# One wide matmul for both activation parts in the up projections, and a whole PSUM bank for each output chunk

## The reference

```python
# block 1: D_FF = 8192
u = _rmsnorm(h, norm_mlp_g[layer])
a = jnp.einsum('bsd,df->bsf', u, w_up[layer])
a = jnp.square(jax.nn.relu(a))
h = h + jnp.einsum('bsf,fd->bsd', a, w_down[layer])

# block 2: D_FF_2 = 5504 = 43 * 128
u = jnp.einsum('btd,df->btf', h, w_up)
u_gate, u_val = jnp.split(u, 2, axis=-1)
g = lax.conv_general_dilated(u_gate.reshape(b, rows, cols, D_FF_2), conv_w[:, :, None, :], ...)  # 3x3 depthwise
g = g.reshape(b, t, D_FF_2) + conv_b
return jnp.einsum('btf,fd->btd', jax.nn.silu(g) * u_val, w_down)
```

## Time and profile before

| | |
|---|---|
| median of 3 runs | 2585.89 us (2580.50 to 2589.67) |
| the profiled execution: its own time | 2585.03 us |
| the profiled execution: span from first to last instruction | 2583.3 us |
| PE busy | 2503.9 us, 97% of the span |
| DVE busy | 1671.1 us, 65% |
| ACT busy | 1080.1 us, 42% |
| DMA | 532.2 MB, mean 206 GB/s |

### The profile page before, as it was taken

The page is one execution under the profiler, slowest core; times in us unless marked ns, Lnnn a source line. Parts: engine busy times, 40 slices in busy tenths (PEclk is TensorE's granted clock), DMA queues, the critical chain, the costliest instruction groups (busy, mean ns, idle before and its releaser), DMA issues.

```text
span 2583.3 us, 36773 instructions
## 1 busy us (share of the span) xinstructions
PE 2503.9 (97%) x14876; PEld 2198.4 (85%) x14876; DVE 1671.1 (65%) x2051; ACT 1080.1 (42%) x1318; POOL 0.2 (0%) x4
## 2 busy tenths in 40 slices
PE   8998999999999999999899999889899999999997
PEld 6886789899899899878678887678899889988996
DVE  5434587867877876654158745766677657775675
ACT  5434544343434344554154444334433434333333
POOL 0000000000000000000000000000000000000000
PEclk9999999999999999999999999989999999999999
DMA  7661567887887887556649866016466665666563
GB/s 281 193 194 49 195 236 265 286 275 275 285 279 269 285 279 258 166 170 191 225 160 354 316 194 208 1 58 189 122 184 181 186 203 182 181 184 188 182 181 127
DMA packets 133365, 532.20 MB, mean 206 GB/s; under 512 B 14944, under 2 KB 14944, under 8 KB 121840
## 3 DMA queue, kind: packets, MB, share of 16 engines
q1 hardware_dynamic: 133232, 530.31, 62.7%
HBM read 528.16 MB, written 2.10 MB: 205 GB/s over the span
## 4 chain that ended last, share of the span: by engine, by line
PE 92%; DVE 5%; ACT 1%; issue 1%; DMA 1%; ACTq 0%; SPq 0%; DVEq 0%
PE PSA L568 28%; PE PSA L570 28%; PE PSA L569 28%; PE PSA L693 1%; DVE cv L1486 1%; PE PSA L1016 1%; PE PSA L724 1%; PE PSA L736 1%; DVE XX L1779 1%; PE PSA L577 0%; PE PSA L1017 0%; PE PSA L904 0%; DVE wlo L1516 0%; PE PSA L871 0%; PE PSA L855 0%
## 5 line engine op out<-in xcount | busy, mean ns | idle before, releaser
L1516 DVE TENSOR_TENSOR wlo<-raw,whi 128x1024 fp32r<-128x1024 f32 x788 | 927.8, 1218 | 423.5 <-ACT whi L1096 420.5
L1096 ACT ACTIVATE whi<-raw 128x1024 fp32r<-128x1024 f32 x788 | 798.3, 1052 | 576.1 <-DMA raw<-in_w_down 212.3
L568 PE MATMUL PSA<-uhi,whi 128*128 128x256 f32 x2400 | 679.5, 283 | 1.0 <-DVE ulo L1629 1.0
L569 PE MATMUL PSA<-ulo,whi 128*128 128x256 f32 x2400 | 679.2, 283 | 0.0
L570 PE MATMUL PSA<-uhi,wlo 128*128 128x256 f32 x2400 | 679.2, 283 | 0.0
L568 PEld LDWEIGHTS PSA<-uhi,whi 128*128 128x128 f32 x2400 | 460.8, 192 | 1.4 <-DVE ulo L1629 1.2
L569 PEld LDWEIGHTS PSA<-ulo,whi 128*128 128x128 f32 x2400 | 460.8, 192 | 0.2
L570 PEld LDWEIGHTS PSA<-uhi,wlo 128*128 128x128 f32 x2400 | 460.7, 192 | 0.0
L568 PE MATMUL PSA<-whi,uhi 128*128 128x512 f32 x1088 | 429.2, 395 | 3.2 <-DVE zl L1879 2.2
L569 PE MATMUL PSA<-wlo,uhi 128*128 128x512 f32 x1088 | 427.0, 392 | 0.0
L570 PE MATMUL PSA<-whi,ulo 128*128 128x512 f32 x1088 | 426.8, 392 | 0.0
(11 more groups left out here) (275 smaller groups left out, 1531.0 us busy)
## 6 DMA issues: line engine op xcount, KB each, us to landing
raw<-in_w_up SPq DMA_DIRECT2D x300, 512.0 KB, 3.6
raw<-in_w_in SPq DMA_DIRECT2D x208, 512.0 KB, 3.9
raw<-in_w_down SPq DMA_DIRECT2D x192, 512.0 KB, 3.6
mod_slot<-in_w_mod_rows SPq DMA_DIRECT2D x78, 1024.0 KB, 6.2
raw<-in_w_out SPq DMA_DIRECT2D x64, 512.0 KB, 3.6
raw<-in_w_mod SPq DMA_DIRECT2D x36, 512.0 KB, 4.4
raw<-in_w_down2b SPq DMA_DIRECT2D x20, 512.0 KB, 3.9
h<-in_x SPq DMA_DIRECT2D x2, 1024.0 KB, 6.1
```

What stands on the lines that cost most here:

```text
L568: pe.matmul(dst, xh, wh, start=start, stop=False)
L569: pe.matmul(dst, xh, wl, start=False, stop=False)
L1096: AF(whi[:, n % SLOTS, 0:w], raw[:, n % SLOTS, 0:w], ACT.Copy).then_inc(hi_done, 1)
L1516: TT(wlo[:, n % SLOTS, 0:w], raw[:, n % SLOTS, 0:w], whi[:, n % SLOTS, 0:w], ALU.subtract).then_inc(lo_done, 1)
```

## The change

- `uhi` and `ulo` become the two halves of one tensor `u2` (for each of 16 k: 256 high columns, then 256 low columns), with views under the old names, and `u_pair` is the view with both side by side (512 columns). The bytes of all k cover the same addresses as before.
- In a feat tile, high weights times `u_pair` is one matmul of 512 columns, and low weights times `uhi` stays one of 256. A tile is 8 + 8 matmuls instead of 24. The sum of high*high and low*high is in columns 0 to 255 of the bank, high*low in columns 256 to 511, so each output chunk has a bank of its own and a block 4 banks. Feat blocks alternate between banks 0 to 3 and 4 to 7 (`Phase.bank`).
- The two halves must be added at readout. ACT copies the second half out of PSUM (`AF(low, ...)`, into `sq` in up1, into the new `vlow` in up2) as soon as PE has ended the block, and DVE adds it to the first half. In up1 this add takes the place of the max, and ACT does a relu in place ahead of the square. In up2 the add writes the new SBUF tensor `gv`, and the convolution and the product with `sl` read `gv` instead of PSUM; the banks come free after the add.
- The gate rows of the second MLP and their copies move from `up2_0` to `dn2_0`: the matmuls behind PE's tile 3, the copies behind DVE's first split of the second block.

```diff
-        uhi = at("uhi", [P, KD, TOK], F32R)
-        ulo = at("ulo", [P, KD, TOK], F32R)
+        u2 = at("u2", [P, KD, 2, TOK], F32R)
+        uhi, ulo = u2[:, :, 0, :], u2[:, :, 1, :]
+        u_pair = u2[:, :, :, :].rearrange("p k w t -> p k (w t)")
...
+    def bank(self, b):
+
+        return 4 * ((b + self.high) % 2) if self.kind == "feat" else 4 * self.high + 2 * (b % 2)
...
                                 f, half = t // 2, t % 2
-                                dst = acc[:, 2 * buf + f // 2, (f % 2) * TOK:(f % 2 + 1) * TOK]
+                                both, main = PSA[:, b0 + f, :], PSA[:, b0 + f, 0:TOK]
                                 for kk in range(8):
                                     k = 8 * half + kk
                                     c = slice(kk * P, (kk + 1) * P)
-                                    mm = product(dst, wh[:, c], wl[:, c], uhi[:, k, :], ulo[:, k, :], k == 0, k == KD - 1)
+                                    if k < KD - 1:
+                                        pe.matmul(both, wh[:, c], u_pair[:, k, :], start=k == 0, stop=False)
+                                        mm = pe.matmul(main, wl[:, c], uhi[:, k, :], start=False, stop=False)
+                                    else:
+                                        pe.matmul(main, wl[:, c], uhi[:, k, :], start=False, stop=False)
+                                        mm = pe.matmul(both, wh[:, c], u_pair[:, k, :], start=False, stop=True)
...
+            def gate_rows_5():
+                pe.wait_ge(mini_done, BY["out2"].unit0)
+                pe.wait_ge(acc_free, BY["dn2_0"].blk0)
+                gate_rows(5 * KD, 0)
...
-                               between={(1, 0): lambda: (pe.wait_ge(u_ready, 48), gate_rows(5 * KD, 4))} if p.name == "up2_0" else {})
-                stream(BY[f"dn2_{g}"], a0=4 * GROUPS1 + 8 * g)
+                stream(BY[f"dn2_{g}"], a0=4 * GROUPS1 + 8 * g, between={(0, 3): gate_rows_5} if g == 0 else {})
...
+                if p.kind == "feat":
+                    low = sq[:, :].rearrange("p (f t) -> p f t", f=4) if p.evac == "up1" else vlow[:, 0:p.main // 2, :]
+                    act.wait_ge(tile_used, end)
+                    if p.evac == "up1":
+                        if not isinstance(nb, int) or int(p.name[4]) * 4 + nb:
+                            act.wait_ge(a_ready, int(p.name[4]) * 4 + nb)
+                    else:
+                        act.wait_ge(acc_free, p.blk0 + nb)
+                    AF(low, PSA[:, b0:b0 + p.main // 2, TOK:2 * TOK], ACT.Copy).then_inc(low_copied, 1)
                 if p.evac == "up1":
                     ab = int(p.name[4]) * 4 + nb + 1
                     act.wait_ge(acc_free, p.blk0 + nb + 1)
+                    AF(rl[:, :], rl[:, :], ACT.Relu).then_inc(act_sq, 1)
+                    act.wait_ge(act_sq, 2 * ab - 1)
                     AF(sq[:, :], rl[:, :], ACT.Square).then_inc(act_sq, 1)
...
                 if p.evac == "up1":
                     dve.wait_ge(tile_used, end)
-                    TS(rl[:, :], acc[:, 2 * buf:2 * buf + 2, :], 0.0, None, ALU.max).then_inc(acc_free, 1)
+                    dve.wait_ge(low_copied, F0[p.name] + nb + 1)
+                    TT(rl[:, :].rearrange("p (f t) -> p f t", f=4), PSA[:, b0:b0 + 4, 0:TOK], sq[:, :].rearrange("p (f t) -> p f t", f=4), ALU.add).then_inc(acc_free, 1)
                 if p.evac == "up2":
...
-                    gate = [acc[:, 2 * buf + n, 0:TOK].rearrange("p (r c) -> p r c", c=64) for n in range(w)]
+                    dve.wait_ge(low_copied, F0[p.name] + nb + 1)
+                    TT(gv[:, 0:2 * w, :], PSA[:, b0:b0 + 2 * w, 0:TOK], vlow[:, 0:2 * w, :], ALU.add).then_inc(acc_free, 1)
+                    dve.wait_ge(acc_free, p.blk0 + nb + 1)
+                    gate = [gv[:, 2 * n, :].rearrange("p (r c) -> p r c", c=64) for n in range(w)]
...
-                    TT(sv[:, 0:w, :], acc[:, 2 * buf:2 * buf + w, TOK:2 * TOK], sl[:, 0:w, :], ALU.mult).then_inc(acc_free, 1)
+                    TT(sv[:, 0:w, :], gv[:, :, :].rearrange("p (n w) t -> p n w t", w=2)[:, 0:w, 1, :], sl[:, 0:w, :], ALU.mult).then_inc(sv_done, 1)
```

More of the change, by code:

```diff
@@ L77, with __init__ @@
 class Phase:
-    def __init__(self, name, kind, iters, blocks, main, k=None, evac=None, dest=0, mods=(), mods_from=0, mods_to=None):
+    def __init__(self, name, kind, iters, blocks, main, k=None, evac=None, dest=0, mods=(), mods_from=0, mods_to=None, high=False):
         self.name, self.kind, self.iters, self.blocks = name, kind, iters, blocks
@@ L88, in __init__ @@
         assert iters == 1 or self.per_iter % SLOTS == 0
+        self.high = int(high)
         assert self.mods_per_iter % 2 == 0
+        assert iters == 1 or blocks % 2 == 0
+    def bank(self, b):
+        return 4 * ((b + self.high) % 2) if self.kind == "feat" else 4 * self.high + 2 * (b % 2)
     def cuts(self):
@@ L136, in plan @@
     for q in range(GROUPS1):
-        ph.append(Phase(f"up1_{q}", "feat", 2, 2, 8, evac="up1", mods=MIXED))
-        ph.append(Phase(f"dn1_{q}", "tok", 2, 2, 8, k=16, evac="res", mods=MIXED if q < GROUPS1 - 1 else ()))
+        ph.append(Phase(f"up1_{q}", "feat", 2, 2, 8, evac="up1", mods=MIXED, high=q % 2 == 0))
+        ph.append(Phase(f"dn1_{q}", "tok", 2, 2, 8, k=16, evac="res", mods=MIXED if q < GROUPS1 - 1 else (), high=q % 2 == 0))
     ph.append(Phase("inC", "tok", 3, 2, 8, k=KD, evac="zc", dest=6))
@@ L364, in program @@
         h_final = sem("h_final")
-        act_sq, a_hi, cv_done, sl_done = (sem(n) for n in ("act_sq", "a_hi", "cv_done", "sl_done"))
+        act_sq, a_hi, cv_done, sl_done, sv_done = (sem(n) for n in ("act_sq", "a_hi", "cv_done", "sl_done", "sv_done"))
+        low_copied = sem("low_copied")
         blk2 = {n: sem(n) for n in (
@@ L411, in program @@
             at_ += steps(p) * p.iters * p.blocks
+        F0, at_ = {}, 0
+        for p in STREAMS:
+            if p.kind == "feat":
+                F0[p.name] = at_
+                at_ += p.iters * p.blocks
         A0, at_ = {}, 0
@@ L628, in body @@
                         nblk = p.blk0 + b + i * p.blocks
-                        buf = b % 2 if p.blocks % 2 == 0 else p.blk0 % 2
+                        b0 = p.bank(b)
                         new = first and b == 0
@@ L652, in body @@
                                         s_ = slice(tt * P, (tt + 1) * P)
-                                        mm = product(acc[:, 2 * buf + tt, :], xh[:, k, s_], xl[:, k, s_], wh[:, c], wl[:, c], k == 0, k == p.k - 1)
+                                        mm = product(PSA[:, b0 + tt, :], xh[:, k, s_], xl[:, k, s_], wh[:, c], wl[:, c], k == 0, k == p.k - 1)
                             else:
                                 f, half = t // 2, t % 2
-                                dst = acc[:, 2 * buf + f // 2, (f % 2) * TOK:(f % 2 + 1) * TOK]
+                                both, main = PSA[:, b0 + f, :], PSA[:, b0 + f, 0:TOK]
                                 for kk in range(8):
@@ L1032, in _ @@
                     if p.name.startswith(f"up2_{g}"):
-                        stream(p, u0=40 if p.name == "up2_0" else None,
-                               between={(1, 0): lambda: (pe.wait_ge(u_ready, 48), gate_rows(5 * KD, 4))} if p.name == "up2_0" else {})
-                stream(BY[f"dn2_{g}"], a0=4 * GROUPS1 + 8 * g)
+                        stream(p, u0=40 if p.name == "up2_0" else None)
+                stream(BY[f"dn2_{g}"], a0=4 * GROUPS1 + 8 * g, between={(0, 3): gate_rows_5} if g == 0 else {})
         @block.scalar
@@ L1060, in evacuate @@
                 nb = i * p.blocks + b
-                buf = (b % 2) if p.blocks % 2 == 0 else p.blk0 % 2
+                b0 = p.bank(b)
                 if p.evac in ("z1", "zc", "zl"):
@@ L1064, in evacuate @@
                     z = {"z1": z1[:, :, :].rearrange("p t (n c) -> p t n c", c=512), "zc": zc, "zl": zl}[p.evac]
-                    AF(z[:, 0, nb, :], acc[:, 2 * buf, :], ACT.Copy)
-                    AF(z[:, 1, nb, :], acc[:, 2 * buf + 1, :], ACT.Copy).then_inc(acc_free, 1)
+                    AF(z[:, 0, nb, :], PSA[:, b0, :], ACT.Copy)
+                    AF(z[:, 1, nb, :], PSA[:, b0 + 1, :], ACT.Copy).then_inc(acc_free, 1)
                 if p.name in SUMMED:
@@ L1440, in evacuate @@
                     if p.name in PARTED:
-                        TT(hb[:, 0, :], acc[:, 2 * buf, :], hb[:, 0, :], ALU.add).then_inc(h_part, 1)
-                        TT(hb[:, 1, :], acc[:, 2 * buf + 1, :], hb[:, 1, :], ALU.add).then_inc(acc_free, 1)
+                        TT(hb[:, 0, :], PSA[:, b0, :], hb[:, 0, :], ALU.add).then_inc(h_part, 1)
+                        TT(hb[:, 1, :], PSA[:, b0 + 1, :], hb[:, 1, :], ALU.add).then_inc(acc_free, 1)
                     else:
-                        TT(hb, acc[:, 2 * buf:2 * buf + 2, :], hb, ALU.add).then_inc(acc_free, 1)
+                        TT(hb, PSA[:, b0:b0 + 2, :], hb, ALU.add).then_inc(acc_free, 1)
                 if p.evac == "gres":
@@ L2018, in _ @@
```

(2 more changed lines are left out.)

20 lines of the change are left out of this document (11 added, 9 removed).

## The result

The changed kernel took 2592.22 us (median of 20 runs, 2587.15 to 2598.47), the kernel before 2586.65 us (20 runs). The ratio is 1.0028, with a 95% interval of 1.002 to 1.0036: 0.28% slower, where I had forecast 2576 us, 0.38% faster, and a range up to 2588. The profiled execution has a span of 2590.7 us against 2583.3, 7.4 us more.

The account below looks back on a forecast made before the run. PE, busy 97% of the span, bounds the kernel through matmul cost and waits for splits. Terms -31.4 + 17.4 + 0.8 + 2.0 - 0.9 + 2.4 + 0.5 = -9.2 us gave 2576 us; 8-in-10 range 2564 to 2588.

Parts of the forecast that it names:

- the price of the wide matmul: Up products: one 512-column matmul at 226.9 ns (bounds 226.9 and 232.8) replaces two of 120.0; -31.4 us over 2400.
- the fixed part: Each matmul on PE costs 13.1 ns beside its columns, the same for 256 and 512 columns.
- Rival 2: Up tiles: the wide matmul takes 232.8 ns, as with `ahi`; sum +0.5, 2586 us, no change; chance 0.10.
- The chain: In up2, from PE's last matmul through readout to the next weight split: 1.96 us longer unrolled, 2.05 in a loop.
- The waits: PE stalls for the up2 readout: 12 x 1.45 = +17.4 us in loops, `dn2_1` +2.0, `dn2_0` -0.9, into `dn2_2` +2.4.
- the cost of 0: In up1, splits come 2.14 us later and DVE's later readouts run late, yet PE does not wait: 0 us.

Follow-up runs that it names:

- the wide matmuls alone: Changed kernel without the low-weight matmuls of the up projections, so an up tile is 8 wide matmuls in a row; mean distance 227.3 to 227.8 ns in up1.
- The grouped kernel: Changed kernel with each up tile's matmuls reordered as 8 wide together and 8 narrow together; 2589.33 us, ratio 0.9999 to the kernel before.
- groups of four: Changed kernel with an up tile's matmuls ordered four wide, four narrow; `up1_1` 89.81 us, 350.8 ns a pair.
- The readout alone: Changed kernel with the wide matmul taken apart into narrow ones, three per product, new readout kept; 2603.11 us, ratio 1.006 to the kernel before.
- groups of two: Changed kernel with an up tile's matmuls ordered two wide, two narrow; `up1_1` 89.37 us, 349.1 ns a pair.

## Why the prediction was wrong

**The step that failed is the price of the wide matmul.** I took 226.9 ns from rows in which every matmul is 512 columns wide, and added 120.0 from rows in which every one is 256 wide, on the ground that the fixed part of 13.1 ns was the same in both. Each was right for a run of its own kind (the wide matmuls alone, 227.3 to 227.8 ns), but the sum was not right for the two in turn: 352.9 ns a pair instead of 346.9, with 235.7 for the wide one. The term was -31.4 us and is 2400 x 7.1 ns = -17.0 us. The grouped kernel, whose pair costs 347.9 ns, gives most of it back. What in TensorE makes the mix dearer no run shows.

**Rival 2 had the size of the miss, for another reason.** It put the wide matmul at 232.8 ns, 5.9 ns dearer; the pair was 6.0 dearer. Its sum was +0.5 us, the measured one +7.4. The rest, 6.9 us, is small things of one sign, none of which the prediction had: 1.1 us in the `dn1` phases, 0.8 us outside the streams, 2.3 us in the `dn2` phases, and about 2.7 us in up2. Most of the part in `dn2` is the two stretches at 1.2 GHz: 1.5 us in `dn2_1` (93.94 us, against 92.38 with groups of four, which waited 2.85 us at the same place and had no such stretch) and 0.7 us in `dn2_2`. The part in up2 is spread over its blocks and goes in part to a longer chain. So even rival 2 had no more than the wide matmul right; with this step alone mended the sum would have said no change, where the kernel is 0.28% slower.

**The chain.** I forecast 1.96 us of growth unrolled; `dn2_1` resumed 14.22 us after its start (2306.75 - 2292.53) against 12.06, so it was 2.16. ACT's copy took 1.03 us and the add 1.23, as counted. The two tensor_scalar operations fell from 0.99 to 0.74 us, 0.26 (995 to 735 ns) and not 0.35: they take 410 ns each, not the 350 of the earlier trace rows, which was another operation; the second one starts 0.33 us after the first, where it was 0.46. The estimate that the prediction worked out from the Trainium skill ("VectorE: DVE Perf Modes", "Mode 2×_2P — use both read ports for one tensor"), 267 ns for the pair, was the better one, and the trace agrees with it within 10 ns. In a loop the chain grew by 2.11 (15.39 from the 13.28 of the prediction), forecast 2.05.

**The waits were right in place and number.** Twelve in the loops, of 1.1 to 1.4 us where 1.45 was forecast, since the dearer pair makes the five tiles that cover the chain 0.24 us longer; the wait into `dn2_1` of 2.2 us more; none in `dn2_0`, where the gate rows cover it (92.9 us, forecast 92.8). The readout alone cost 15.1 us against 14.8 by the same sum, in part by luck, as said above.

**Up1.** DVE did fall behind as described: it waited only 0.18 us, for ACT's copy, ahead of the later readouts of each phase. Two of the four readouts of `up1_1`, in DVE's timeline of the changed kernel:

```profile
619.74 1.23 DVE L1501 TENSOR_TENSOR rl<-PSA,sq 128x1024 f32<-128x1024 f32 x1 [0.18 <-ACT sq L1103]
...
642.35 1.23 DVE L1501 TENSOR_TENSOR rl<-PSA,sq 128x1024 f32<-128x1024 f32 x1 [0.18 <-ACT sq L1103]
```

PE has no wait from 368 to 1000 us, so the cost of 0 was right. It holds at the speed that was forecast too: the grouped kernel, with blocks of 22.27 us, has no wait of PE there either.

**The fixed part.** The rule of the Trainium skill, about 2.5 ns beside the columns ("TensorE: Matmul & The Clock Gate", "Wait — 56ns, not 53.3ns?"), does not hold for any of these fp32r matmuls. By its rule the columns alone take 213.3 ns (512) and 106.7 ns (256) at 2.4 GHz; beside them the traces show 13.3 to 13.5 ns (up, and in and out before), 19 (down), and 33 for a wide and a narrow one in turn. My mistake was to read the constancy of two of these numbers as a law for a third case.

**The chances.** A difference of less than 0.3% either way had 0.30, and the 0.28% slower lies just within it; 0.57 was on faster by more. The time of 2592 us is above the range of 8 in 10, which ended at 2588. The forecast rested on a margin of 2 us, and the one price that no row showed was taken at the cheaper of its two bounds for all 2400 products, with 0.10 for the dearer.

## What to carry to other kernels

A distance between matmuls taken from a run of equal ones was at best a lower bound here, not a price, for a mix; where 2400 of them hang on 6 ns, measure the mix in the order in which it will run, and try the order too. Work added to a readout is paid by the tiles that cover it: count the chain from PE's last matmul to the first split behind it against the tiles that PE has left, and move the readout when the chain grows. A change whose gain and loss are on different limits should be tried with its loss cured (here the place of the readout and the order of the matmuls) before it is judged: 0.3% slower became 1.2% faster. And an experiment that is worth a few microseconds is read from the phases that it touches: the time of the whole moved by as much where nothing was changed.

## What the runs showed of the hardware

- The same 16 matmuls took 5.0 ns a pair more one by one than in eights (352.9 and 347.9), and groups of four took more than groups of two (350.8 and 349.1). One by one the wide one took 235.7 ns and the narrow one 117.2, where runs of equal ones take 227 and 120.0. The cause is open.
- Where an operand starts in SBUF changes the distance of fp32r matmuls: 64 bytes moved 512-column ones from 226.8 to 233.3 ns (`u` as the stationary operand), or from 232.4 to 228.9 (`ahi`), and 256-column ones from 120.0 to 117.8. Why is open as well.
- The same wait of PE at the same place was followed by a stretch at 1.2 GHz in some kernels and not in others. In `dn2_1` it came after 2.91 us in the changed kernel and 2.90 in the readout alone, but not after 2.90, 2.90 and 2.85 us with groups of eight, two and four. Ahead of `dn2_2` it came after 2.5 to 2.9 us in all of these but groups of two. It never came after the twelve waits of 1.1 to 1.4 us a block apart, nor after the 0.75 us before. So a forecast of a wait near 3 us should carry some 0.7 to 1.5 us of lower clock as a possible extra.
